# Expert rows gathered earlier, and two more places for them, in a one-core transformer kernel

## The reference

```
q = (t @ wq)                                 # 8 heads, 2 halves
s = q against 2 x 128 sub-keys per head
s1, i1 = top_k(s[..., 0], 16); s2, i2 = top_k(s[..., 1], 16)
top, pos = top_k(s1[:, None] + s2[None, :], 16)        # 16 experts per head
idx = i1 * 128 + i2 at pos
g = softmax(top)
a = gelu(einsum('tpkd,td->tpk', u[idx], t))            # rows of u
return einsum('tpk,tpkd->td', g * a, v[idx])           # rows of v
```

## Time and profile before

| | us |
|---|---|
| median of 3 runs | 2861.39 |
| lowest, highest of them | 2847.32, 2865.62 |
| time of the profiled execution | 2850.39 |
| its span (first to last instruction) | 2848.5 |
| PE, DVE, ACT, POOL busy in the span | 2307.4, 1885.7, 903.9, 1095.7 |

### The profile page before, as it was taken

One profiled execution on the slowest core, in us unless ns is written; L12 is line 12 of the kernel. 1 busy time (PEld: TensorE's weight loads), 2 busy tenths in 40 slices (PEclk: granted clock), 3 DMA queues, 4 the chain that ended last, 5 costly groups with the idle time before them and its releaser, 6 DMA issues.

```text
span 2848.5 us, 43514 instructions
## 1 busy us (share of the span) xinstructions
PE 2307.4 (81%) x16384; PEld 1723.0 (60%) x16384; DVE 1885.7 (66%) x4182; ACT 903.9 (32%) x1615; POOL 1095.7 (38%) x1029
## 2 busy tenths in 40 slices
PE   7999988877455564665757989766999999999998
PEld 5788876445311110113646877523777899997998
DVE  3666885787565666457898877663444587677766
ACT  4556652111100000001023334322423455457544
POOL 0000002544466666667786665676556000000000
PEclk8999999988787776877969999867999999999999
DMA  7432126797799999999999999999999545662554
GB/s 301 151 129 85 38 83 247 279 350 294 289 375 378 365 368 352 358 354 345 409 344 403 401 408 409 408 360 362 363 405 395 208 153 194 190 208 90 186 188 152
DMA packets 225231, 810.32 MB, mean 284 GB/s; under 512 B 24704, under 2 KB 30720, under 8 KB 223232
## 3 DMA queue, kind: packets, MB, share of 16 engines
q0 software_dynamic: 147456, 536.94, 49.3%
q1 hardware_dynamic: 76992, 270.09, 26.5%
q10 hardware_dynamic: 576, 0.52, 0.1%
HBM read 805.35 MB, written 2.10 MB: 283 GB/s over the span
## 4 chain that ended last, share of the span: by engine, by line
PE 39%; DVE 17%; issue 10%; DMA 8%; another core or an unknown queue 6%; POOL 3%; ACT 1%; DVEq 0%; POOLq 0%; SPq 0%; ACTq 0%
PE ps L2005 10%; PE ps L2006 9%; PE ps L2007 9%; DVE pe_ring L2848 6%; PE ps L1940 5%; DMA pe_ring<-in_v,pe_vidx 4%; DMA pe_ring<-in_u,pe_idx 1%; POOL pe_ring L1827 1%; PE ps L1895 1%; DVE pe_itop L2775 1%; POOL pe_ring L1833 1%; DVE la_w_lo L2901 1%; DVE pe_top L2771 1%; DMA la_k<-in_v,pe_vidx 1%
## 5 line engine op out<-in xcount | busy, mean ns | idle before, releaser
L1827 POOL DMA_INDIRECT pe_ring<-in_u,pe_idx x415 | 463.8, 1118 | 293.0 <-issue 113.3
L1940 PE MATMUL ps<-pe_ring,pe_spot 128*32 128x512 f32 x1620 | 386.9, 752 | 199.2 <-DMA pe_ring<-in_v,pe_vidx 140.9
L1833 POOL DMA_INDIRECT pe_ring<-in_v,pe_vidx x405 | 426.5, 1053 | 221.5 <-issue 116.4
L2005 PE MATMUL ps<-la_h_hi,la_w_hi 128*128 128x256 f32 x1696 | 483.4, 285 | 12.1 <-DVE la_w_lo L2901 6.7
L2007 PE MATMUL ps<-la_h_hi,la_w_lo 128*128 128x256 f32 x1696 | 477.8, 282 | 1.7 <-issue 1.7
L2006 PE MATMUL ps<-la_h_lo,la_w_hi 128*128 128x256 f32 x1696 | 477.6, 282 | 1.6 <-issue 1.5
L2901 DVE TENSOR_TENSOR la_w_lo<-la_w_raw,la_w_hi 128x1024 fp32r<-128x1024 f32 (+1 forms) x348 | 415.5, 1195 | 78.0 <-ACT la_w_hi L2470 64.1
L2470 ACT ACTIVATE la_w_hi<-la_w_raw 128x1024 fp32r<-128x1024 f32 (+1 forms) x348 | 359.5, 1033 | 295.4 <-DMA la_w_raw<-in_down 78.7
L2005 PEld LDWEIGHTS ps<-la_h_hi,la_w_hi 128*128 128x128 f32 x1696 | 323.2, 191 | 47.8 <-issue 31.7
L1940 PEld LDWEIGHTS ps<-pe_ring,pe_spot 128*32 128x32 f32 x1620 | 76.9, 125 | 411.9 <-issue 313.1
L2007 PEld LDWEIGHTS ps<-la_h_hi,la_w_lo 128*128 128x128 f32 x1696 | 320.3, 189 | 2.2 <-issue 2.1
(11 more groups left out here) (409 smaller groups left out, 3899.2 us busy)
## 6 DMA issues: line engine op xcount, KB each, us to landing
la_w_raw<-in_gate SPq DMA_DIRECT2D x88, 512.0 KB
la_w_raw<-in_up SPq DMA_DIRECT2D x88, 512.0 KB
la_w_raw<-in_down SPq DMA_DIRECT2D x64, 448.0 KB
la_w_raw<-in_a_in SPq DMA_DIRECT2D x40, 512.0 KB
wring<-in_w_in SPq DMA_DIRECT2D x32, 512.0 KB
la_w_raw<-in_down SPq DMA_DIRECT2D x32, 512.0 KB
wring<-in_wq SPq DMA_DIRECT2D x22, 512.0 KB, 7.5
xT<-in_w_mod_rows SPq DMA_DIRECT2D x8, 1024.0 KB, 4.9
```

The source lines that it names most:

```text
L1827: pool.indirect_dma_start(row(n), None, io["u"], bass.IndirectOffsetOnAxis(idx[:, t, j:j + 1], 0)).then_inc(land[GATHERS[n][0]], 16)
L1833: pool.indirect_dma_start(row(n), None, io["v"], bass.IndirectOffsetOnAxis(vidx[:, t % 2, at:at + 1], 0)).then_inc(land[GATHERS[n][0]], 16)
L1940: return pe.matmul(ps[PER * grp:PER * grp + PER, half, :], spot[:, j // TOKENS % 2, grp, lo:lo + PER], row(n)[:, half * 512:(half + 1) * 5 ...
L2005: pe.matmul(slot(n), parts_hi[:, n % SPLIT, i, :], hi[:, k, :], start=first, stop=False)
```

## The change

There are two parts. The first is in `gathers()`: 28 u rows of tile 2 (`EARLY`) stand between the last 28 v rows of tile 1, four and four. DVE makes these 28 dots right after `choose(3, 3)`, ahead of `half(0)`. All of `half(0)`'s indices into tile 2's dots move up by 28, as do the origin of the due times and the number of dots that read the tokens from PSUM (36 where it was 8). `LAST` becomes 468.

```
+SCRATCH = 8192
+SPARE = (16384 - SCRATCH) // (4 * D)
...
-            consts_in, x_in, mod_in = sem("consts_in"), [sem(f"x_in{n}") for n in range(3)], [sem(f"mod_in{u}") for u in range(4)]
+            consts_in, x_in, mod_in = sem("consts_in"), [stage_sem(f"x_in{n}") for n in range(3)], [sem(f"mod_in{u}") for u in range(4)]
...
+    more_rows = sb("pe_more_rows", [P, SPARE, D], on=local)
...
-    HEAD, IN_PSUM = 26, 8
+    EARLY, HEAD, IN_PSUM = 28, 26, 8
...
-        for j in range(P):
+        for j in range(P - EARLY):
             yield "v", 1, j
-        for j in range(P):
+        for j in range(0, EARLY, GROUPS):
+            for k in range(j, j + GROUPS):
+                yield "u", 2, k
+            for k in range(j, j + GROUPS):
+                yield "v", 1, P - EARLY + k
+        for j in range(EARLY, P):
             yield "u", 2, j
...
-        return TURN[kind, t, j] - TURN["u", 2, HEAD] + LAG
+        return TURN[kind, t, j] - TURN["u", 2, EARLY + HEAD] + LAG
...
+    MORE += [(RING + 10 + k, 0, len(ORDER)) for k in range(SPARE)]
...
-                elif n and slot >= RING + 6:
+                elif n and RING + 6 <= slot < RING + 10:
                     pool.wait_ge(dot_done, (slot - RING - 3) * HK)
...
-                within_psum = t < 2 or t == 2 and j < IN_PSUM
+                within_psum = t < 2 or t == 2 and j < EARLY + IN_PSUM
...
-                for j in range(HEAD, HK):
+                for j in range(EARLY + HEAD, HK):
                     yield used_at("u", 2, j)
                     dot(2, j)
...
-                    for j in range(3):
+                    for j in range(EARLY, EARLY + 3):
                         dot(2, j)
...
+            for j in range(EARLY):
+                dot(2, j)
             beside = Beside(dots_beside(), weights_beside(), sums_beside())
             half(0, beside)
...
-    nc = bacc.Bacc("TRN2", target_bir_lowering=False, num_devices=1)
+    nc = bacc.Bacc("TRN2", target_bir_lowering=False, num_devices=1, dynamic_dma_scratch_size=SCRATCH)
```

More of the change, by code:

```diff
@@ L1504, in program @@
     MORE += [(TOKEN_SLOTS[t], LENT_AT, TOKENS_AT if t else P) for t in reversed(range(TT))] + [(TOKEN_SLOTS[t], TURN["v", t, 16], len(ORDER)) for t in (2, 3)]
+    MORE += [(RING + 10 + k, 0, len(ORDER)) for k in range(SPARE)]
     row_spaces = ([ring[:, k, :] for k in range(RING)] + [within("hT", f"pe_more{k}", k * D, [P, D])[:, :] for k in range(4)]
-                  + [kT[:, :, :].rearrange("p a n -> p (a n)"), v[:, :, :, :].rearrange("p c t n -> p (c t n)"), htok[:, 2, :], htok[:, 3, :], htok[:, 1, :], htok[:, 0, :]])
+                  + [kT[:, :, :].rearrange("p a n -> p (a n)"), v[:, :, :, :].rearrange("p c t n -> p (c t n)"), htok[:, 2, :], htok[:, 3, :], htok[:, 1, :], htok[:, 0, :]]
+                  + [more_rows[:, k, :] for k in range(SPARE)])
     land = [sem(f"pe_land{k}") for k in range(len(row_spaces))]
@@ L3105, in half @@
                     add_sum(1, 1)
-                    for j in range(3, 8):
-                        dot(2, j)
-                    for j in range(8, 16):
+                    for j in range(EARLY + 3, EARLY + 16):
                         dot(2, j)
@@ L3113, in half @@
                         if k % 2:
-                            dot(2, 16 + k // 2)
-                    for j in range(20, HEAD):
+                            dot(2, EARLY + 16 + k // 2)
+                    for j in range(EARLY + 20, EARLY + HEAD):
                         dot(2, j)
```

## The result

In one comparison on one chip the changed kernel takes 2871.1 us (median of 14 runs, 2856.9 to 2888.9) and the kernel before 2856.5 (14 runs, 2847.3 to 2869.2). The ratio is 1.0062, with a 95% interval of 1.0045 to 1.0080: slower by 18 us by the ratio (the two medians lie 14.7 us apart), measurably, and by less than one percent. The forecast was 2865 us and "within one percent" the likeliest class. Of the change itself it had forecast only +7 us; several terms behind that were off and partly cancelled.

A forecast was written before the change was run, and what follows sets the result against it. Transferred rows were taken to bound the kernel up to about 1960 us, PE's work from 2000. Terms 40 + 11 - 8 - 5 = 38, less 31, gave +7 us on the runs' mean: 2865 us, range 2832 to 2893.

The forecast's parts named there:

- A: End of tile 1: 28 more rows ahead of the last v row, at 1.43 us each, issue it 40 us later.
- B: End of tile 1: POOL's 23rd gather waits for the first early row's dot after choose(3, 3), +11 us, bounds 0 and 25.
- E: half(0): 28 fewer rows beside PE's products give time back, -31 us, at least -20 and at most -49.
- C: End of tile 1: DVE, done choosing, is no longer late; last v row to scale_x 30 us, -8 us, bounds 0 and 12.
- D: Before 1254 us: two more ring places let POOL fetch more rows during holds, -5 us, from 0 to 10 gained.
- DVE works on rows as they arrive: End of tile 1: with the choice done, 16 rows take 23 us, plus 6 for landing and 1.2 for the dot.
- the rival in which POOL was the bound: half(0)'s first stage: POOL's issuing sets 1.75 us a row; half(0) gains up to 49 us, total -25, 2833 us; chance 0.14.
- the second rival's counter-argument: half(0): ticks are fixed, so what the first stage loses in rows the DMA-bound stage gains in weight tiles.
- the full hold: End of tile 1: choice gets no faster, DMA engines run dry for 25 us, little given back; +38 us, 2896; chance 0.18.
- POOL as the bound of the first stage: half(0), 1339.6 to 1550 us: POOL's issuing, not DMA, prices a row at 1.75 us; total -25 us; chance 0.14.
- The descriptors: 405 GB/s stage: half the descriptor space is too little, rate falls to 360, +37 us and more, about 2902; chance 0.04.
- Nothing happens: Whole kernel: DMA engines stay busy, same bytes, the queue covers the hold and the terms cancel at 2858 us; chance 0.06.

The follow-up runs named there:

- e1: Changed kernel without the early u rows, keeping the two more ring places and the halved descriptor space; ratio to the kernel before 1.0045.
- e5: Changed kernel without early u rows, its two more places opened only from tile 1's first u row; ratio to the kernel before 1.0006.
- e3: Kernel before with only the descriptor space halved to 8192 bytes; ratio to the kernel before 1.0001.
- e6: Changed kernel with POOL paused, before the fourth gather behind tile 1's last v row, until PE has summed tile 1; ratio to the kernel before 1.0077.

## Why the prediction was right, and where not

The class and the range held, and so did terms A, B and E of the early rows in kind. Terms C and D had the wrong sign. That 2871 us came so near to 2865 is luck in part: the forecast for the change alone was +7 us, less than half of the 18 measured, and it would have been further off had E not been too small as well.

- **A, right.** The 56 gathers take 94.2 us with a hold of 15.7: 94.2 - 15.7 - 39.9 = 38.6, forecast 40.
- **B, right in kind, a little small.** 15.7 us where 11 stood, ended by the named dot. Other executions had 13.9 to 24.5, so the bounds of 0 and 25 were needed. The reason given for 11 fits: the choice shrank to 17.4 us with POOL held.
- **C, wrong.** From the last v gather to `scale_x` 42.9 us instead of 30. Take the unnamed wait of 12.1 us out and 30.8 are left, so the steps were priced well and the wait was missed. The failed step is "DVE works on rows as they arrive": PE's and ACT's handover was taken as free, as it had been in the one profile at hand, where DVE was still choosing.
- **D, wrong sign.** The 100th v row was forecast at about 1249 and came at 1259.7 (1253.0 before; this is a stretch in which profiles differ by 6 us for nothing, so the ratios say more). e1 puts the price of the two places at +13 us against -5 forecast, and e5 puts all of it that can be measured before tile 1's u rows. The argument looked only at what POOL gains from a place. It didn't ask what the others lose while POOL uses it.
- So `half(0)`'s first product came at 1405.2 us, not 1378. The 27 us are 12 of D, 13 of C, 5 of B, less 1 of A, within 2.
- **E, right in kind, too small.** From the first product to the end it is 1468.0 us instead of 1508.9, 40.9 less (forecast 31), 1.46 for each of the 28 rows moved. 452 gathers follow the first product (458 forecast), 33 fewer than before by the same count, since POOL went on during the unnamed wait. To the last v sum it is 42.3 us less, 1.28 for each of the 33 where 1.11 was taken. Up to the first v row of tile 2 the stage gave back 62.8 us, 1.9 a row, near the 1.75 of the rival in which POOL was the bound. Up to the first v row of tile 3, 6 to 17 us were lost again (against e3 and before). That fits what the second rival's counter-argument said of the fixed ticks.
- **The sum.** +66 and -41 where +38 and -31 stood: +25 in the profiles and +18 by the ratio instead of +7. Errors of +27 and -10 cancelled in part.

Of the rivals, the full hold didn't come in this execution. e6 has its length, 24.5 us, but not its mechanism: the choice took 15.0 us there and only began late. POOL as the bound of the first stage shows in its rate but not in the sum. The descriptors are excluded by e3, with 406 to 408 GB/s in the stretch that was to tell. "Nothing happens" fell as well. The doubled issue times of the earlier trace rows are seen again, up to 1.99 us while the dots read `pe_htok`. By the Trainium skill, "SBUF — State Buffer", Who interferes with whom, a DVE instruction with two SBUF inputs contends with a GpSimd one that reads SBUF, and the trace agrees. The limit of about 358 GB/s that the Trainium skill, "DMA: Bandwidth & Descriptors", gives in its Specifications is passed here too: 408 GB/s over 300 us.

## What to carry to other kernels

A deeper ring of prefetched rows is not free where the engines that make room for them are late: each row issued ahead lengthened another engine's handover by about one transfer, and four places fewer in one stage gained 12 us where two more had lost 13. So ask for every extra place what waits while POOL fills it, test the depth of a ring stage by stage and in both directions, and before pricing a handover at nothing look at it in several profiles. Moving transfers out of a busy stage does pay back close to one transfer each, but that must outweigh what delays the stage's start: 12 rows were neutral, 28 were not.

## What the runs showed of the hardware

- At the start of the gathers a signal from PE ended ACT's wait later by 1.4 us for each row (128 x 1024 floats, by indirect DMA) that POOL had issued in one go: 5.2, 8.1, 10.8 and 16.4 us of wait for 5, 7, 9 and 13 rows. Whether the rows or POOL's issuing hold it back is open.
- `choose(3, 3)`, the same small instructions of DVE each time, took 15 to 17 us in the four profiles with POOL held at the first early row and 23 to 32 in the ten others. Before and after, the difference is mostly waits without a named releaser (14.3 and 2.3 us). POOL's issuing alone does not make a choice long: `choose(2, 2)` before took 17.9 us, `choose(3, 2)` after 16.9.
- Half the descriptor space, 8192 bytes a partition, made no difference that could be measured: ratio 1.0001 with 20 places (e3), 1.0006 with 22 from tile 1's u rows on (e5).
- Times of the same kernel before were 2856 us on one chip and 2870 to 2872 on others. Only comparisons on one chip could tell 0.4%.
